# Decoder trunk on one core: where ScalarE takes projection blocks out of PSUM, makes the rotary tables, and where VectorE scales the second block of heads

## What is computed

```
h = rmsnorm(x, g_norm) @ w_in                       # (256, 3072)
qa, ka, va, qb, kb, vb = split(h)                   # six blocks of 512 = 4 heads of 128
o_sb  = stick_breaking(rmsnorm(qa), rmsnorm(ka), va)
qb, kb = apply_rope(rmsnorm(qb), cos, sin), apply_rope(rmsnorm(kb), cos, sin)
o_dil = dilated_attention(qb, kb, vb)
x = x + concat(rmsnorm(o_sb), rmsnorm(o_dil)) @ w_out
```

## Time and profile before

| | us |
|---|---|
| median of 3 runs | 1922.3 |
| lowest, highest | 1922.09, 1926.2 |
| the profiled execution, its own time | 1924.84 |
| span of the profiled execution | 1922.8 |
| TensorE busy | 1907.9 |
| VectorE busy | 1348.2 |
| ScalarE busy | 1161.4 |
| GpSimd busy | 136.7 |

### The profile page before, as it was taken

One profiled execution on the slowest core, in us unless ns is written; L12 is line 12 of the kernel. 1 busy time (PEld: TensorE's weight loads), 2 busy tenths in 40 slices (PEclk: granted clock), 3 DMA queues, 4 the chain that ended last, 5 costly groups with the idle time before them and its releaser, 6 DMA issues.

```text
span 1922.8 us, 25622 instructions
## 1 busy us (share of the span) xinstructions
PE 1907.9 (99%) x8984; PEld 1589.0 (83%) x8984; DVE 1348.2 (70%) x1574; ACT 1161.4 (60%) x1490; POOL 136.7 (7%) x152
## 2 busy tenths in 40 slices
PE   9999999999999999999999999999999999999998
PEld 7788888888888888888888888888888888888887
DVE  8786654544555445445658688898989889899896
ACT  7556534334443334334645567788887878787885
POOL 8300000000000000000200000010000100000101
PEclk9999999999999999999999999999999999999999
DMA  9555565666656566665565468999999999999997
GB/s 356 177 162 155 182 188 186 192 192 191 190 188 196 187 190 193 191 192 187 182 191 165 154 209 304 387 394 386 393 384 393 391 391 381 400 381 402 375 397 258
DMA packets 141570, 510.13 MB, mean 265 GB/s; under 512 B 15936, under 2 KB 15952, under 8 KB 140080
## 3 DMA queue, kind: packets, MB, share of 16 engines
q1 hardware_dynamic: 134288, 486.64, 71.0%
q0 software_dynamic: 7200, 22.39, 4.6%
HBM read 495.33 MB, written 13.64 MB: 265 GB/s over the span
## 4 chain that ended last, share of the span: by engine, by line
PE 96%; DVE 1%; DMA 1%; ACT 1%; issue 0%; POOLq 0%; SPq 0%; DVEq 0%; ACTq 0%
PE main L617 31%; PE main L619 30%; PE main L618 30%; DMA raw_pieces<-in_ffn_moe 1%; PE transpose L951 1%; PE transpose L635 1%; PE transpose L816 0%; DVE w_low L1391 0%; PE transpose L991 0%; PE transpose L657 0%; PE transpose L934 0%; ACT w_high L1052 0%; ACT token_major L1307 0%; PE spread L679 0%; DMA token_major<-in_x_t 0%
## 5 line engine op out<-in xcount | busy, mean ns | idle before, releaser
L1391 DVE TENSOR_TENSOR w_low<-raw_pieces,w_high 128x1024 fp32r<-128x1024 f32 x919 | 1095.5, 1223 | 424.6 <-ACT w_high L1052 418.1
L1052 ACT ACTIVATE w_high<-raw_pieces 128x1024 fp32r<-128x1024 f32 x919 | 949.3, 1058 | 259.9 <-DMA raw_pieces<-in_ffn_dense 127.8
L617 PE MATMUL main<-w_high,xT_high 128*128 128x512 f32 (+1 forms) x1856 | 720.9, 388 | 1.3 <-DVE w_low L1512 1.1
L619 PE MATMUL main<-w_high,xT_low 128*128 128x512 f32 (+1 forms) x1856 | 711.4, 383 | 0.0
L618 PE MATMUL main<-w_low,xT_high 128*128 128x512 f32 (+1 forms) x1856 | 710.7, 383 | 0.0
L619 PEld LDWEIGHTS main<-w_high,xT_low 128*128 128x128 f32 x1856 | 349.5, 188 | 68.4
L617 PEld LDWEIGHTS main<-w_high,xT_high 128*128 128x128 f32 x1856 | 349.9, 188 | 66.6 <-DVE xT_low L1418 1.3
L618 PEld LDWEIGHTS main<-w_low,xT_high 128*128 128x128 f32 x1856 | 350.0, 189 | 64.8
L617 PE MATMUL main<-w_high,hT_high 128*128 128x512 f32 x832 | 330.4, 397 | 0.9 <-DVE hT_low L1785 0.9
L619 PE MATMUL main<-w_high,hT_low 128*128 128x512 f32 x832 | 325.1, 391 | 0.0
L618 PE MATMUL main<-w_low,hT_high 128*128 128x512 f32 x832 | 324.6, 390 | 0.0
(11 more groups left out here) (231 smaller groups left out, 812.1 us busy)
## 6 DMA issues: line engine op xcount, KB each, us to landing
raw_pieces<-in_ffn_moe SPq DMA_DIRECT2D x528, 512.0 KB, 6.3
raw_pieces<-in_ffn_dense SPq DMA_DIRECT2D x264, 512.0 KB, 3.5
raw_pieces<-in_w_in SPq DMA_DIRECT2D x96, 512.0 KB, 3.6
raw_pieces<-in_w_out SPq DMA_DIRECT2D x32, 512.0 KB, 3.5
x_resid<-in_x SPq DMA_DIRECT2D x4, 512.0 KB, 14.6
out_x<-x_resid POOLq DMA_DIRECT2D x4, 512.0 KB, 3.7
xn_rows<-token_major POOLq DMA_DIRECT2D x2, 1024.0 KB, 5.5
token_major<-in_x_t SPq DMA_DIRECT2D x1, 1024.0 KB, 9.6
```

The lines of the kernel that those rows point to most:

```text
L617: pe.matmul(out_ap, lh[ls], rh[rs], start=first, stop=False)
L619: return pe.matmul(out_ap, ll[ls], rh[rs], start=False, stop=last)
L1052: act.activation(WH[:, piece % RING, :], RAWS[:, piece % RING, :], ACT.Copy).then_inc(high_done, 1)
L1391: dve.tensor_tensor(WL[:, piece % RING, :], RAWS[:, piece % RING, :], WH[:, piece % RING, :], ALU.subtract).then_inc(low_done, 1)
```

## The change

Three edits, all in the mixer loops:

1. ScalarE takes blocks 1 to 5 out as the first thing in slots 16, 24, 32, 40 and 48, ahead of `high` of that slot and of its attention steps. Block 0 stays where it was, in slot 8. The semaphores waited for are the same. This holds in both layers.
2. Sine and cosine move from ScalarE's slot 12 to slot 18, and the load of the table for logarithm and exponential from slot 13 to slot 18, right behind the cosine (layer 0 alone).
3. VectorE scales block 1 in slot 17 instead of 18 (both layers), that is behind one `low` fewer.

```diff
-V_SCALE = {10: (0, (0, 1)), 18: (1, (0, 1)), 26: (2, (0,)), ...}
+V_SCALE = {10: (0, (0, 1)), 17: (1, (0, 1)), 26: (2, (0,)), ...}
...
+                def block_out(c):
+
+                    act.wait_ge(used, m["piece"] + (c + 1) * IN_PIECES)
+                    for t in range(TILES):
+                        act.activation(QKV[:, t, IN_ORDER[c] * NB:(IN_ORDER[c] + 1) * NB], PAIR[c % 2][t][:, :], ACT.Copy,
+                                       scale=RSTD[2 * layer][:, t:t + 1]).then_inc(gu_free, 1)
+
                 for i in range(MIX_PIECES):
...
+                    if i > IN_PIECES and i % IN_PIECES == 0 and i <= W_OUT0:
+                        block_out(i // IN_PIECES - 1)
                     high(m["piece"] + i + LEAD)
...
-                        if i == 12:
+                        if i == 18:
                             act.wait_ge(rope_red, 1)
                             act.activation(SIN[:, :, :], RED, ACT.Sin).then_inc(tables_done, 1)
                             act.activation(COS[:, :, :], TURN, ACT.Sin).then_inc(tables_done, 1)
...
-                    if i == (13 if layer == 0 else T_ROOT - 1):
+                    if i == (18 if layer == 0 else T_ROOT - 1):
                         act.preload_act_table_set("natural_log_exp_and_others")
...
-                    if i and i % IN_PIECES == 0 and i <= W_OUT0:
-                        c = i // IN_PIECES - 1
-                        act.wait_ge(used, m["piece"] + i)
-                        if c == 0:
-                            act.wait_ge(rstd_done, 2 * layer + 1)
-                        for t in range(TILES):
-                            act.activation(...).then_inc(gu_free, 1)
+                    if i == IN_PIECES:
+                        act.wait_ge(rstd_done, 2 * layer + 1)
+                        block_out(0)
```

More of the change, by code:

```diff
@@ L74 @@
 V_SQ = {8: 0, 16: 1, 24: 2, 32: 3}
-V_SCALE = {10: (0, (0, 1)), 18: (1, (0, 1)), 26: (2, (0,)), 27: (2, (1,)), 34: (3, (0,)), 35: (3, (1,))}
+V_SCALE = {10: (0, (0, 1)), 17: (1, (0, 1)), 26: (2, (0,)), 27: (2, (1,)), 34: (3, (0,)), 35: (3, (1,))}
 V_SP, V_AZ = {21: 0, 24: 1, 29: 2, 32: 3}, {23 + 4 * h: h for h in range(HEADS)}
@@ L1204, in mixer @@
                         act.activation(WDT[A_WT[i]], U[1][:, 0:3 * P], ACT.Copy).then_inc(wt_done, 1)
-                    if i and i % IN_PIECES == 0 and i <= W_OUT0:
-                        c = i // IN_PIECES - 1
-                        act.wait_ge(used, m["piece"] + i)
-                        if c == 0:
-                            act.wait_ge(rstd_done, 2 * layer + 1)
-                        for t in range(TILES):
-                            act.activation(QKV[:, t, IN_ORDER[c] * NB:(IN_ORDER[c] + 1) * NB], PAIR[c % 2][t][:, :], ACT.Copy,
-                                           scale=RSTD[2 * layer][:, t:t + 1]).then_inc(gu_free, 1)
+                    if i == IN_PIECES:
+                        act.wait_ge(rstd_done, 2 * layer + 1)
+                        block_out(0)
                     if i in A_ROOT:
```

## The result

| | median, us | lowest to highest, runs | ratio to before, 95% interval |
|---|---|---|---|
| before | 1925.52 | 1922.09 to 1928.14, 11 | |
| after | 1929.43 | 1928.50 to 1931.80, 11 | 1.0023 [1.0015, 1.0031] |
| before, second comparison | 1926.03 | 1922.70 to 1928.13, 25 | |
| after, second comparison | 1928.88 | 1928.19 to 1931.70, 11 | 1.0019 [1.0010, 1.0028] |

The change makes the kernel slower by 0.19 to 0.23%, +4.4 and +3.7 us by the ratios and +3.9 and +2.9 us by the medians. The intervals are +2.9 to +6.0 us and +1.9 to +5.4 us. The time lies inside the range, at its upper end, and the outcome of the first comparison was not the one forecast as likeliest.

What follows compares the result with a forecast made beforehand. TensorE, busy 1907.9 of 1922.8 us, was taken as the bound, its largest idle stretch 3.3 us in layer 0. -3.5 + 0.5 + 4 x 1.45 = +2.8 us on the 1922.3 median gave 1925.1 us, range 1922.0 to 1929.5.

Steps and rivals of the forecast that it cites:

- the range: Whole kernel: forecast time between 1922.0 and 1929.5 us, leaving out the clock falling three times or more.
- Part 1: Layer 0, slot 18: block 1 out earlier, TensorE's long wait shrinks, scores start sooner: -3.5 us, bounds -4.3 and -2.8.
- Part 2: Layer 1, same moves without sines: low part of slot 16 waits behind the block, turn later: +0.5 us, bounds 0 and 1.
- Parts 3 and 4: Blocks 2 and 3 before the softplus, slots 24 and 32: TensorE waits 1.45 us longer in slots 30 and 37, both layers.
- Part 5: Blocks 4 and 5, GpSimd's rope tables, SyncE's queue and ring: taken at nothing; block 4 up to 1.45 us per layer.
- the rope tables: GpSimd starts them near 61.8 instead of 60.6, VectorE wants them in slot 26: taken at no cost.
- the ring: SyncE's queue and ring: a high part up to 2 us later, six pieces before its use, taken at no cost.
- The clock at a new wait: Rival, slots 30 and 37: clock falls behind the longer waits, up to 1.48 us each; one fall gives +4.3; chance 0.32.
- Its second form: Clock rival, slot 18: unprofiled runs keep 2.4 GHz before the change, only 2.0 us can be gained, +4.3 in all.
- No new waits: Rival: VectorE absorbs 1.45 us twice in each layer, total -3.0 us, 1919.3; chance 0.10.
- block 1 no earlier: Rival, slot 18: ScalarE reaches slot 16 late for another reason, total +6.3 us, 1928.6; chance 0.04.
- Drained tables: Rival, slot 18: ScalarE needs 2.7 us more for two table switches before the copies, +5.5 us, 1927.8; chance 0.04.

Runs made afterwards that it cites:

- second comparison: The changed kernel, unchanged, timed a second time on another chip against the kernel before: 1928.88 us, ratio 1.0019.
- blocks 2 and 3 back: The changed kernel with blocks 2 and 3 taken out where they were before, behind softplus and exponential: 1922.55 us, ratio 0.9987 against before.
- The blocks alone: The kernel before with blocks 1 to 5 taken out first in their slots, sines in slot 12, scaling in slot 18: 1936.67 us, ratio 1.0061.
- before_look5: The kernel before, unchanged, in its sixth profile, with late angles: own time 1924.17 us.
- the sines alone: The kernel before with only the sines and the table load behind them moved to slot 18: 1921.44 us, ratio 0.9981.
- blocks 2 and 3 alone: The kernel before with only blocks 2 and 3 taken out in front of the high part, slots 24 and 32: 1931.15 us against 1926.03, ratio 1.0028.

## Why the prediction was right or wrong

**Part 1, slot 18 of layer 0: the mechanism right, the size right for one course only. This is the step that failed.** Block 1 came out at 52.40 (forecast 52.45), the turn at 60.95 (61.1), the scores at 64.88 (65.05), with the two small waits where they were said to be (0.42 and 0.55, forecast 0.7 and 0.7). Against the profiled execution that is -3.7, forecast -3.5. But that execution had late angles and a low clock. Over the six profiles of before the scores start at 68.57, 68.46, 68.62, 65.26, 65.98 and 66.91, 67.30 in the mean; over three of after at 65.04. **The term measured -2.3 and not -3.5**, uncertain by about 0.6; with all timed runs, +3.8 us in total, it would be -2.5, and from blocks 2 and 3 back (-2.5 by the ratio) -3.0. The sum was made against one execution. It took the 2.46 us wait of ScalarE for the angles in rows 5 and the low clock behind TensorE's wait as fixed, and the gain rests on these two. Of six profiles two had no wait for the angles, and a third had it but kept the full clock. With -2.3 the sum reads -2.3 + 0.5 + 5.8 = +4.0. That the term is smaller than -3.5 in other executions is shown; its exact mean, and so the whole of the missing microsecond, is not.

**Part 2, layer 1:** the turn now waits 0.42, forecast +0.5.

**Parts 3 and 4, the four waits:** 1.45 forecast; the idle times ahead of PE's steps are 1.47 and 1.45 in layer 0 and 1.45 and 1.46 in layer 1. The reasons hold too: the softplus late by what doesn't fit into ScalarE's idle time, and VectorE with no slack to give back. Putting the high part first gave two thirds back.

**Part 5, the edits at nothing:** no wait appears for blocks 4 and 5, the rope tables or the ring.

**The rivals.** The clock at a new wait: the rival's own mechanism never came. In all three profiles of after it is at 1.00 behind all four waits of 1.45 to 1.48. Its second form, that runs without a profile keep the high clock in before so that less can be gained, was half right: in one of four late profiles the clock did stay up, at a cost to the change of 1.6 us in that form. That one was a profiled execution too, so profiling by itself does not bring the low clock. No new waits, and block 1 no earlier: both refuted by the rows above. Drained tables: behind the second load the next high part starts 1.29 us after the load (61.75, 63.04). The Trainium skill (ScalarE: Activation LUTs, What ACT_TABLE_LOAD costs) would have a drain of about 1.38 us on top, and these rows have no room for it. The Trainium skill (TensorE: Matmul & The Clock Gate, Part 1) says that idleness throttles the engine and activity releases it. The blocks alone show a second case of that, behind 1.99 us, but the wait of 3.12 us in `before_look5` throttled nothing.

**From the sum to the outcome.** Two further steps made it worse. The median of three runs, 1922.3, was taken as the base, though one of the three was at 1926.2; 11 runs gave 1925.52, so the forecast time of 1925.1 started 3.2 too low. And +2.8 lay 1.0 below the 3.8 us set as the border of "same", while the unknown of the clock reached only upwards. The gain of part 1 had been priced at its full value and could mainly shrink, so "slower" deserved at least even odds; this is judged afterwards. Even now the size, 0.19 and 0.23%, sits on that border. That the first pair of traces came out at +2.8 says little for the size of the sum: it was worked out from the very execution of before that it is compared with.

## What to carry to other kernels

Before a wait is counted as a gain, follow it back to its first cause and ask whether that cause has the same time in every execution: a chain that starts with small loads and a slow engine may not, and one profile shows one draw. A block taken out first in its slot waits there for TensorE and holds up work that used to run in that idle time. Here the softplus was late by 1.45 us, more than the 1.15 us of the block itself: 1.15 for the block and 0.95 for the high part, less the 0.65 us of idle time that was left. Put it behind what can run in the idle time. Try each edit of a bundle alone: here the sines alone gain 4.5 us by the medians, and blocks 2 and 3 alone lose 5.1, while the bundle lost 3.9 and 2.9.

## What the runs showed of the hardware that I had not expected

- The clock does not follow from the length of one wait. It fell behind waits of 1.99, 2.85, 3.12, 3.26, 3.31 and 4.12 us and did not behind another one of 3.12 us, nor behind any of the waits of 1.45 to 1.48 us in the changed kernel's three profiles. Where it fell, 4.7 to 4.8 us passed from turn to scores instead of 3.2.
- The same program on the same data has a GpSimd chain of 50 us whose last step started at 44.06, 46.49 or 48.19 to 48.44 in six executions. Single steps of it differ by 0.9 us (1.23 and 2.09).
- Two table loads inside a busy stretch of ScalarE cost 1.30 and 1.29 us from start to next start (59.92 to 61.22 and 61.75 to 63.04), with no further gap.
